# One gather of 16 KB expert rows in place of separate U and V gathers, in a PEER layer on one core

## What is computed

```python
q = (ut @ w_q).reshape(T, PEER_HEADS, 2, D_KEY // 2)
s = einsum('thpd,pnd->thpn', q, sub_keys)          # two halves of 128 keys
top_s, top_i = top_k(s, 16)
cand_s = top_s[:, :, 0, :, None] + top_s[:, :, 1, None, :]
cand_i = top_i[:, :, 0, :, None] * N_KEYS + top_i[:, :, 1, None, :]
best_s, best_j = top_k(cand_s, 16);  idx = cand_i[best_j];  g = softmax(best_s)
act = gelu(einsum('cd,chkd->chk', x, U[idx])) * g
y = einsum('chk,chkd->cd', act, V[idx])
```

## Time and profile before

| | us |
|---|---|
| median of the runs | 2310.98 (2310.67 to 2313.8) |
| the profiled execution, device time | 2317.97 |
| its span, first to last instruction | 2316.1 |
| TensorE matmul busy | 2066.1 (89%) |
| VectorE busy | 1480.5 (64%) |
| GpSimd busy | 759.2 (33%) |
| ScalarE busy | 576.6 (25%) |
| DMA traffic | 808.28 MB, mean 349 GB/s |

### The profile page before, as it was taken

The page is one execution under the profiler, slowest core; times in us unless marked ns, Lnnn a source line. Parts: engine busy times, 40 slices in busy tenths (PEclk is TensorE's granted clock), DMA queues, the critical chain, the costliest instruction groups (busy, mean ns, idle before and its releaser), DMA issues.

```text
span 2316.1 us, 22827 instructions
## 1 busy us (share of the span) xinstructions
PE 2066.1 (89%) x7550; PEld 1334.8 (58%) x7550; DVE 1480.5 (64%) x2111; ACT 576.6 (25%) x1113; POOL 759.2 (33%) x764
## 2 busy tenths in 40 slices
PE   3999999999999999999987887888788888888987
PEld 3888999977888887887433333333333333333333
DVE  6837767868876556688256656664666568565544
ACT  0014454463443333422111111111111111112010
POOL 0001010011111000056565555455555444555562
PEclk9999999999999999999989899888888888889988
DMA  9946676666998665699999999999999999999996
GB/s 395 420 184 247 227 262 217 230 244 243 386 335 289 218 221 182 253 379 398 366 421 422 422 422 422 422 422 421 422 421 422 422 422 421 421 422 418 418 411 267
DMA packets 126789, 808.28 MB, mean 349 GB/s; under 512 B 14197, under 2 KB 14581, under 8 KB 39285
## 3 DMA queue, kind: packets, MB, share of 16 engines
q0 software_dynamic: 92160, 604.02, 63.9%
q1 hardware_dynamic: 34264, 202.70, 23.4%
q10 hardware_dynamic: 288, 0.53, 0.1%
HBM read 805.10 MB, written 2.10 MB: 349 GB/s over the span
## 4 chain that ended last, share of the span: by engine, by line
PE 52%; DMA 21%; DVE 10%; POOL 6%; issue 6%; ACT 4%; POOLq 0%; DVEq 0%; ACTq 0%; SPq 0%
PE ps L617 52%; DMA front<-in_peer_u,arena 16%; DVE front L2023 3%; DMA front<-in_ada_first 3%; DVE arena L1517 2%; POOL arena L558 2%; POOL front L550 1%; POOL arena L550 1%; POOL arena L538 1%; DMA front<-in_peer_v,arena 1%; DMA arena<-in_peer_v,arena 1%; POOL front L558 1%; POOL front L604 0%; ACT front L1148 0%; DVE split_ring L1670 0%
## 5 line engine op out<-in xcount | busy, mean ns | idle before, releaser
L617 PE MATMUL ps<-arena 128*128 128x512 f32 (+3 forms) x2670 | 968.9, 516 | 231.5 <-ACT arena L1330 178.2
L617 PEld LDWEIGHTS ps<-arena 128*128 128x128 f32 x2670 | 509.1, 207 | 670.0 <-issue 491.8
L2023 DVE CUSTOM_DVE_ANT_0 front<-front,arena 128x2048 f32<-128x2048 f32 x180 | 409.5, 2292 | 200.6 <-DMA front<-in_peer_u,arena 195.5
L617 PE MATMUL ps<-front,arena 128*128 128x512 f32 (+1 forms) x832 | 355.9, 576 | 1.9 <-DMA front<-in_peer_v,arena 1.9
L2023 DVE CUSTOM_DVE_ANT_0 arena<-arena 128x2048 f32<-128x2048 f32 x60 | 137.5, 2296 | 266.2 <-DMA arena<-in_peer_u,arena 261.0
L617 PEld LDWEIGHTS ps<-front,arena 128*128 128x128 f32 x832 | 157.6, 190 | 191.1 <-issue 185.9
L550 POOL DMA_INDIRECT front<-in_peer_u,arena x176 | 239.2, 1359 | 68.4 <-issue 45.7
L1318 ACT ACTIVATE arena<-arena 128x4 f32<-128x4 f32 x64 | 13.2, 207 | 906.7 <-DVE arena L2003 906.6
L1670 DVE TENSOR_TENSOR split_ring<-front,split_pada 128x2048 fp32r<-128x2048 f32 x72 | 164.9, 2291 | 100.3 <-ACT split_pada L1207 99.9
L538 POOL COPY arena<-arena 128x4 uint32 (+1 forms) x120 | 82.6, 688 | 380.2 <-PE ps L617 357.2
L509 POOL DMA_DIRECT2D arena<-in_w_ada x64 | 34.0, 532 | 479.1 <-DVEq L1582 190.5
(11 more groups left out here) (256 smaller groups left out, 2565.6 us busy)
## 6 DMA issues: line engine op xcount, KB each, us to landing
front<-in_w_in_u SPq DMA_DIRECT2D x64, 1024.0 KB, 7.6
arena<-in_w_ada POOLq DMA_DIRECT2D x128, 512.0 KB, 7.0
front<-in_ada_first SPq DMA_DIRECT2D x32, 1024.0 KB, 11.8
front<-in_w_rnn_out_u SPq DMA_DIRECT2D x16, 1024.0 KB, 6.7
front<-in_w_mla_out_u SPq DMA_DIRECT2D x16, 1024.0 KB, 5.0
front<-in_w_o_u SPq DMA_DIRECT2D x16, 1024.0 KB, 4.9
front<-in_peer_wq_u SPq DMA_DIRECT2D x11, 1024.0 KB, 8.1
arena<-in_peer_wq_u SPq DMA_DIRECT2D x5, 1024.0 KB, 9.1
```

The costliest lines, as they stand in the source:

```text
L617: return pe.matmul(o, l, r, start=start, stop=stop, skip_group_check=True, **k)
L2023: V.tensor_tensor_reduce(uslot[s], uslot[s], h2[T], 1.0, 0.0, ALU.mult, ALU.add, zraw[:, s:s + 1]).then_inc(dots_done, 1)
```

## The change

The host lays the U row and the V row of an expert side by side in one table `peer_uv`. It is read in two ways: as rows of 8 KB (`rows`, U at index 2e, V one row behind it) and as rows of 16 KB (`row_pairs`). Head 0 still gathers its 16 U rows and its 16 V rows one by one from `rows`, 1 MB each; its indices are doubled by topk (`TS(topf, topi, 2.0, ...)`). Heads 1 to 15 gather a U and a V row at once, 128 rows of 16 KB, 2 MB, into one of eight double slots (`pair`), which take the memory of the sixteen slots before. A double slot is free when the product of its expert is done. VectorE's dots no longer run a head ahead: in each head, group by group, come dots, gelu, weights, diagonals and products of the same head. GpSimd issues each gather of a pair as soon as the product eight experts earlier is done, one wait each, and copies indices for four ahead. The second gate moves to `gate2`, and ScalarE makes it after the first group of head 1. In the last head the last four experts are weighed as two, one and one.

```diff
-    for n in ("ln1_g", "ln1_b", "ln2_g", "ln2_b", "peer_u", "peer_v"):
+    for n in ("ln1_g", "ln1_b", "ln2_g", "ln2_b"):
         out[n] = a[n]
+    out["peer_uv"] = np.concatenate([a["peer_u"][0], a["peer_v"][0]], axis=1).reshape(-1, D)
...
-        vslot = [at(R_G + 3 * D, D)] + reused + [pada[0], at(R_HT, D), at(R_HT + D, D)]
+        gate2 = at(R_G + 3 * D, D)
+        vslot = [infront(R_MODS + 3 * D, D)] + reused + [pada[0], at(R_HT, D), at(R_HT + D, D)]
+        pair = [at(R_HG, 2 * D), infront(R_RING, 2 * D), infront(R_RING + 2 * D, 2 * D), infront(R_MODS + 2 * D, 2 * D),
+                infront(R_MODS, 2 * D), at(R_G, 2 * D), infront(R_PADA, 2 * D), at(R_HT, 2 * D)]
...
+        rows = t["peer_uv"]
+        row_pairs = rows.rearrange("(n two) d -> n (two d)", two=2)
...
+            def first_v(e):
+
+                if e < 8:
+                    pool.wait_ge(unit_used, 4 * B_WQ + (11, 12, 13, 14, 15, 16, 16, 16)[e])
+                else:
+                    pool.wait_ge(pv_done, 2 * GROUP + e - 7)
+                pool.indirect_dma_start(vslot[e % 8], None, rows, index_at(e), element_offset=D).then_inc(in_v[e % 8], 16)
+
+            def first_pair(s):
+
+                pool.wait_ge(dots_done, 2 * GROUP + (10, 14, 16, 16, 16, 16, 16, 16)[s])
+                if s >= 3:
+                    pool.wait_ge(pv_done, 2 * GROUP + (9, 11, 13, 14, 16)[s - 3])
+                pool.indirect_dma_start(pair[s], None, row_pairs, index_at(TOPK + s)).then_inc(in_pair[s], 16)
+
+            def pair_group(H, e):
 
                 pool.sem_inc(pool_gate, 1)
-                me.do(pool.tensor_copy(ix[:, e % 8:e % 8 + GROUP], arena[:, bass.ds(H * TOPK + (o_idx + e), GROUP)].bitcast(U32)))
+                me.do(pool.tensor_copy(idx[:, e % 16:e % 16 + GROUP], arena[:, bass.ds(H * TOPK + (o_idx + e), GROUP)].bitcast(U32)))
                 me.wait()
                 pool.sem_inc(pool_gate, 1)
...
+                for i in range(e, e + GROUP):
+                    s = i % 8
+                    pool.wait_ge(pv_done, H * TOPK + (i + 1))
+                    pool.sem_inc(pool_gate, 1)
+                    pool.indirect_dma_start(pair[s], None, row_pairs, bass.IndirectOffsetOnAxis(idx[:, i % 16:i % 16 + 1], 0)).then_inc(in_pair[s], 16)
+
+            pool.wait_ge(topk_ok, 2)
+            first_pair(0)
+            for e in (0, 1):
+                first_v(e)
+            first_pair(1)
+            for e in (2, 3):
+                first_v(e)
+            first_pair(2)
+            for e in range(4, TOPK):
+                first_v(e)
+            for s in range(3, 8):
+                first_pair(s)
...
+            with pool.Fori(1, last) as H:
+                me.enter(H, 1, TOPK // GROUP)
+                for e in range(8, 8 + TOPK, GROUP):
+                    if e == TOPK:
+                        pool.wait_ge(topk_ok, H + 2)
+                    pair_group(H, e)
+                me.leave(last - 1)
+            for e in (8, 12):
+                pair_group(last, e)
...
             def products(H, T, count=TOPK, end=False):
                 for e in range(count):
-                    q = e % (2 * GROUP)
-                    pe.wait_ge(in_v[q], H * 32 + 16 * (e // (2 * GROUP) + 1))
+                    s = e % 8
+                    pe.wait_ge(in_pair[s], pair_landed(H, e))
                     pe.wait_ge(diag_ok, H * TOPK + (e + 1))
                     for j in range(4):
-                        last = mm(ps[:, 4 * T + j, :], diag[q], vslot[q][:, j * 512:(j + 1) * 512], False, end and e == TOPK - 1)
+                        last = mm(ps[:, 4 * T + j, :], diag[s], pair[s][:, D + j * 512:D + (j + 1) * 512], False, end and e == TOPK - 1)
                     last.then_inc(pv_done, 1)
...
+            def head(H, staged=True, first=0):
+                for q in range(first, TOPK // GROUP):
+                    weigh(H, q)
+                    diagonals(H, q)
+                    if q == 0:
+                        gate_exp(H, 1)
+                    if q == 1 and staged:
+                        act.wait_ge(topk_ok, H + 2)
+                        act.sem_inc(act_gate, 1)
+                        stage_scores(H, 2)
...
+            weigh(1, 0)
+            diagonals(1, 0)
+            modulation(3)
+            gate_exp(1, 1)
+            weigh(1, 1)
+            diagonals(1, 1)
+            act.wait_ge(topk_ok, 3)
+            stage_scores(1, 2)
+            head(1, first=2)
...
+            def last_dots(H, T):
+                for q in range(3):
+                    dve.wait_ge(a_ok, H * (TOPK // GROUP) + (q + 1))
+                    for e in range(q * GROUP, (q + 1) * GROUP):
+                        dot(H, T, e)
+                    gelu_of(H, q)
+                dve.wait_ge(a_ok, H * (TOPK // GROUP) + 4)
+                for e0, e1 in ((12, 14), (14, 15), (15, 16)):
+                    for e in range(e0, e1):
+                        dot(H, T, e)
+                    gelu_rows(H, e0, e1)
```

More of the change, by code:

```diff
@@ L222, in build @@
         zs = at(small(8), 8)
-        idxu, idxv = (at(small(8), 8).bitcast(U32) for _ in range(2))
+        idx = at(small(16), 16).bitcast(U32)
         o_gate = small(NT * EXPERTS)
@@ L566, in _ @@
[L566 to L576, removed]
-            last = NT * PH - 1
[L578 to L611, removed]
@@ L612, in _ @@
-            v_group(last, 3)
+                for i in range(e, e + GROUP):
[8 more added lines that the diff above has]
+            first_pair(1)
@@ L1051, in _ @@
                 if T == 0:
-                    products(0, 0)
+                    first_products()
                     pe.wait_ge(sc_out, 12)
@@ L1065, in _ @@
                 else:
-                    products(NT * PH - 1, T, count=TOPK - 2)
-                    last_products(NT * PH - 1, T, 2)
+                    products(NT * PH - 1, T, count=TOPK - 1)
+                    last_product(NT * PH - 1, T)
         @block.scalar
@@ L1329, in diagonals, with last_rows @@
                     act.wait_ge(pv_done, H * TOPK + (e + 1))
+                    act.sem_inc(act_gate, 1)
                     A(diag[e % 8], ident, ACT.Copy, scale=arena[:, bass.ds(H * TOPK + (o_gate + e), 1)]).then_inc(diag_ok, 1)
+            def last_rows(n, e0, e1):
+                H, o = NT * PH - 1, o_gate + (NT * PH - 1) * TOPK
+                act.wait_ge(z_ok, H * (TOPK // GROUP) + 4 + n)
+                me.do(A(zs[:, e0 % 8:e1 % 8 + 1], zu[:, e0 % 8:e1 % 8 + 1], ACT.Sigmoid, scale=GELU_S))
+                me.wait()
+                for e in range(e0, e1 + 1):
+                    last = A(at(o + e, 1), zs[:, e % 8:e % 8 + 1], ACT.Copy, scale=zg[:, e % 8:e % 8 + 1])
+                last.then_inc(a_ok, 1)
+                act.wait_ge(a_ok, H * (TOPK // GROUP) + 6 + n)
+                for e in range(e0, e1 + 1):
+                    act.wait_ge(pv_done, H * TOPK + (e + 1))
+                    A(diag[e % 8], ident, ACT.Copy, scale=at(o + e, 1)).then_inc(diag_ok, 1)
             act.sem_inc(sc_out, 4)
@@ L1368, in _ @@
             stage_scores(0, 2)
-            weigh(0, 0, 2)
-            weigh(0, 0, 3)
+            weigh(0, 2)
+            weigh(0, 3)
             query(2)
             scores_out(2)
-            weigh(0, 1, 0)
-            gate_exp(0, 2)
             query(3)
@@ L1386, in loop @@
                     me.enter(H, first, TOPK // GROUP)
-                    for q in range(TOPK // GROUP):
-                        if q == 0:
-                            act.wait_ge(topk_ok, H + 2)
-                            stage_scores(H, 2)
-                        if q == 1:
-                            gate_exp(H, 2)
-                        weigh(H, 1, q)
-                        diagonals(H, q)
+                    head(H)
                 me.leave(end - first)
@@ L1948, in top_pairs @@
                 me.wait()
-                me.do(V.tensor_copy(topf, topi))
+                if isinstance(H, int) and H == 0:
+                    me.do(TS(topf, topi, 2.0, None, ALU.mult))
+                else:
+                    me.do(V.tensor_copy(topf, topi))
                 hold()
```

140 lines of the change are left out of this document (58 added, 82 removed).

## The result

The changed kernel takes 2330.9 us (median of 6 runs, 2329.4 to 2335.3) against 2312.5 for the kernel before (6 runs, 2310.7 to 2314.5): a ratio of 1.0077 with a 95% interval of [1.0066, 1.0088]. The forecast was 2294 us, faster. The outcome has the other sign and lies above the range. These 34.7 us between two profiled executions are what has to be explained; the medians are 18.4 us apart.

A forecast was written before the change was run, and what follows sets the result against it. DMA time was taken to bound the kernel. 232 pairs of 4.82 us from 1157 put D 17.2 us earlier: 2318.0 - 17.2 = 2300.8, less 7.0 for profiled execution over median, 2294 us; range 2272 to 2327.

The forecast's parts named there:

- What bounds the kernel: From slice 21 on (1157 us) DMA is full, so DMA time sets the end, not any engine.
- D: The time until which data flow: 2292.4 us before the change, forecast at 2275.2, 17.2 us earlier.
- The time of a pair: 2 MB on full DMA engines: 4.97 us before, 4.82 as 16 KB rows, from the load of xT; ends 4.72 and 4.97.
- The decision point: The time of a pair at which gain turns to loss: 4.89 us, 429 GB/s.
- The rival of the unchanged rate: A pair stays at 4.97 us, only the lost start is left: 2329 us, slower than before; chance 24%.
- The rival from the Trainium skill: About 3 cycles overhead per packet: a pair takes 4.94 us, time about 2322 us; no chance of its own.
- The start: Head 1's double slots need both halves; engines full from 1157 us, 8 MB less moved, costing 20 us of DMA time.
- The steady state: Heads with eight double slots: 11.9 us from landing to next data against 19.3, 7 us to spare, cost nothing.
- the rival of slots running dry: DMA stops in each head; with 2 us lost in each of 15 heads the time is 2324 us; chance 14%.
- The end: After the last pair, first gated sum at D + 5.4 to D + 8, before D + 6.5: nothing gained, within 2 us.

The follow-up runs named there:

- e1_rates: A kernel with none of the layer's work, only gathers and loads of different row sizes; 128 gathered rows of 8, 16, 32 KB took 2.48, 4.90, 9.71 us.
- e5_ahead_tail: Changed kernel with heads 0 and 1 gathering U and V apart as before, and the last head's third group weighed in halves: 2306.0 us, ratio 0.9965.

## Why the prediction was wrong

**What bounds the kernel** was right: the DMA engines are full until D in after as well, and every microsecond of D follows from the pairs to go and the time of one.

**The time of a pair** failed, and this is the largest term, 20.6 us. The step was "a pair takes 4.97 x 0.611 / 0.630 = 4.82". Over the whole full stretch a pair takes 4.918, and 4.895 in `e1_rates`. The 0.611 itself was nearly right. The queues of `e1_rates`, 8 KB gathers from 20 to 70 us and 16 KB gathers from 100 to 150:

```profile
q0 software_dynamic: 2902, 21.10, 101.3%
```

```profile
q0 software_dynamic: 1472, 21.50, 100.8%
```

There 1312 rows of 16 KB book 100.8% x 800 / 1312 = 0.615 us each and 2576 rows of 8 KB book 0.315. But these are booked times, and a share above 100% over 900 us can't come from packets booked whole at the two edges: the packets of an engine overlap. The overlap shrinks with the longer rows (101.3 to 100.8%, in the kernel 101.3 to 100.4%), so the booked time of a pair falls by 2.3% where the elapsed time falls by 1.5%. That is 0.04 of the 0.075 us between 4.82 and 4.895. The rest probably comes from the shortness of the 6 us of xT, with packets booked whole at the edges: nine stretches of 6 us in `e1_rates`' loads of 16 KB rows read from 418 to 437 GB/s, for a steady 430. Without the ratio, 8 rows an engine at 0.611 would have given 4.89.

**The decision point** was right and should have weighed more: a pair of 4.89 us, 429 GB/s. The measured pair (4.918) is beyond it, on the losing side, and the ends of this price (4.72, 4.97) lay on both sides of it, on one load of 2 MB. The rival of the unchanged rate had the right sign and the wrong reason: the rate did rise, and that its 2329 us are near the measured time is luck, since the 14.2 us of the rate were lost again at the end (9.6) and in a start dearer than it had (4.5).

**The rival from the Trainium skill**, 3 cycles saved with each packet, gave 2322 us; the saving of a row is larger than that (1.5% of a pair, not 0.6), but with the costs at the start and the end the time lands above it.

**The start** was right in its order and off by 4.5 us in size, with one row misread. GpSimd's issues of after, against the times in the prediction (V0 1049, V3 1072, V8 1098.8, pair 7 at 1150.3, the next at 1154.1):

```profile
1049.51 0.94 POOL L556 DMA_INDIRECT front<-in_peer_uv,arena  x1 [14.60 <-PE ps L603]
...
1072.02 0.94 POOL L556 DMA_INDIRECT arena<-in_peer_uv,arena  x1 [7.75 <-PE ps L603]
...
1095.88 0.94 POOL L556 DMA_INDIRECT front<-in_peer_uv,arena  x1 [6.62 <-PE ps L603]
...
1147.89 0.94 POOL L563 DMA_INDIRECT arena<-in_peer_uv,arena  x1 [5.93 <-PE ps L603]
...
1154.93 3.08 POOL L575 DMA_INDIRECT arena<-in_peer_uv,arena  x1 [5.90 <-PE ps L603]
```

Each gather that waits for a product of head 0 came some 3 us earlier than predicted, because the prediction took the wrong start for these products. TensorE before, ahead of the earlier trace rows, and TensorE after:

```profile
1086.64 8.94 PE L617 MATMUL ps<-arena 128*128 128x128 f32 x32 [1.11 <-ACT arena L1307]
```

```profile
1086.67 5.50 PE L603 MATMUL ps<-arena 128*128 128x128 f32 x24 [1.11 <-ACT arena L1299]
1092.02 10.46 PE L603 MATMUL ps<-front,arena 128*128 128x512 f32 x24
```

The first V slot of before lies in `arena`, so the view merges the 8 records of the first product with the 24 ahead of it; the 3.44 us by which this row is longer are that product. The products began at 1092.0 in both kernels, and the earlier trace rows has the second and third, not the first two. Read so, product 16 ends at 1146.9, and pair 7 would be through at 1153.4 by the prediction's own terms, before the first slot returns at 1154.1, so the queue would have run empty in between and been full from about 1155.7 (1154.1 + 1.6). In the run, pair 7 was issued at 1147.9 and was through at about 1155.2, while the first slot came back at 1154.9, not far from the 1154.1 predicted. Its gather was of the slow kind of the earlier trace rows, 3.08 us on GpSimd, and its first data came at 1158; between them the queue was empty (97 GB/s from 1155 to 1160, above). Full from 1159.2 instead of 1157: 2.2 us. The misread row brought the forecast nearer to this, by luck. The other 2.3 us are the prediction's own rounding: 232 x 4.97 gave 17.6 us for the 4 pairs which it had itself put at 20.

**The steady state** held nearly, but the 7 us of spare can run out when two delays meet. 232 x (4.918 - 4.895) are 5 us for all stalls of the full stretch. The largest dent in the rate is this one; instructions of after around 2020 us:

```profile
2018.63 10.46 PE L603 MATMUL ps<-front,arena 128*128 128x512 f32 x24
...
2019.61 2.77 POOL L575 DMA_INDIRECT arena<-in_peer_uv,arena  x1 [9.47 <-PE ps L603]
```

and its stretches:

```profile
2012.00:2016.00 4.00, 4.00 (x5) 1.51 (x5) 3.24 (x14) 0.84 (x2) 0.00 (x0) 0.50 0.99 420
...
2019.00:2022.00 3.00, 3.00 (x8) 1.33 (x7) 2.97 (x4) 0.00 (x0) 2.39 (x1) 1.00 0.86 366
2022.00:2024.00 2.00, 2.00 (x6) 0.95 (x5) 2.00 (x3) 0.00 (x0) 1.33 (x2) 1.00 0.62 156
```

From the start of the group's last dot (2005.6) to the gather that reuses a slot it is 14.0 us here and 12.2 in an ordinary group (1611.5 to 1623.7). The first diagonal was there at 2010.4, but TensorE was at the row broadcast that stands ahead of this head (`row_broadcast`, four products with 4 rows of weights), the last of which ran partly at the 1.2 GHz level (granted clock 0.50 in the microsecond from 2011). Its weight loads and the first product's:

```profile
2008.11 0.29 PEld L603 LDWEIGHTS ps<-arena 4*128 4x128 f32 x2 [0.76 <-issue]
...
2012.65 0.50 PEld L603 LDWEIGHTS ps<-arena 128*128 128x128 f32 x2 [1.50 <-issue]
```

So the first product began 7.0 us behind the dot and not 5.3 as in that ordinary group; it took 6.0 us, partly at the low level, which is nothing special (5.9 there). The prediction counted the broadcast rows on VectorE alone. A late gather alone costs nothing that shows: in the group of the dot at 1670.2 it came as late, 14.1 us behind the dot, but took 0.96 us on GpSimd, and the queue stayed full (418 GB/s or more in each 2 us from 1684 to 1690):

```profile
1684.31 0.96 POOL L575 DMA_INDIRECT front<-in_peer_uv,arena  x1 [10.76 <-issue]
```

At 2019.6 the gather took 2.77 us on top of being late, and two microseconds went at 156 GB/s. Both dents of `e5_ahead_tail` have the same two parts: gathers 14.8 and 14.2 us behind the dot, of 3.05 and 2.61 us. This happens once in after and not once a head: the rival of slots running dry was a cost of about 2 us and not of 30. What makes a gather on GpSimd slow wasn't isolated. Where the remaining 3 of the 5 us lie wasn't tried.

**The end** failed by 9.6 us. The step was that the product of the last pair meets an idle TensorE, or at most the product before it, with the first gated sum at D + 5.4 to D + 8; it came at D + 15.9. The backlog was in the prediction's own numbers: seven experts at 3.43 us and a slow first one are some 30 us, and they can't start before the fourth row of the third group has landed, 4 pairs (19.6 us) ahead of D, and been weighed. The 2 us between the last bytes and the dot came on top; the earlier trace rows had 1.6 us for the way from issue to data, but no step asked for the way from data to the waiting engine.

So of the 34.7 us the pair is 20.6 (its gain was put at 34.8 us and was 14.2), the start 4.5, and the end 9.6.

## What to carry to other kernels

Price a longer row by a straight line (so much for a MB, so much for a row) fitted to long steady stretches of at least two row sizes, in elapsed time and not in booked time; where only one short stretch has the new size, the gain is an open number, and its decision point is what to weigh. Merging two transfers into one makes the slot need both halves free and the first user wait for both: count what the merged stages can no longer fetch early, at the start of the pipeline above all, and keep the old form there. At the end of a pipeline add up all products that become ready late, not only the last; if they outlast the rows still to come, weigh them in smaller groups.

## What the runs showed of the hardware

- 128 rows on the full DMA engines take 2.41 us a MB and 0.075 us more, for 8, 16 and 32 KB rows in gathers: 422, 430 and 431 GB/s. Loads of 8 and 16 KB rows have the same 422 and 430; loads of 4 KB rows get 411. On a full queue the completion of a transfer costs nothing that shows (2 MB in 8 KB rows with one completion 423, 1 MB 422).
- An indirect gather moves a 16 KB row, and in `e1_rates` a 32 KB row, without losing rate to the length.
- From the last byte of a lone gather to the start of the engine that waits for it are 1.4 to 1.6 us; at the end of a full queue, where single engines finish later, it is 2.4 us from D. With eight transfers in flight this is hidden (422 GB/s, the rate of the line); at the end of the pipeline it is on the path.
- A share of the DMA engines above 1.00 means overlap, not more work: 101.3% with 8 KB rows and 100.8% with 16 KB rows are both a full queue.
